# Gated linear attention: the levels' gaps, decays, splits and unit copies in another order, one pair ahead

## What is computed

```python
def gla_mixer(h, w_in, w_gate2, b_gate, o_norm_g, w_out):
    q, k, v, g, lr = split(h @ w_in)            # 4 heads, dk 128, dv 256; lr: 2 x 16 gate columns
    la_f, la_b = log_sigmoid(lr_d @ w_gate2[d] + b_gate[d]) / 16      # decays, forwards and backwards
    o_f = gla(q / sqrt(128), k, v, la_f)                              # o_i = sum_{j<=i} (q_i exp(b_i - b_j)) . k_j v_j
    o_b = flip(gla(flip q, flip k, flip v, flip la_b, strict))        # the same from behind, j > i
    return (rms_norm(o_f + o_b, o_norm_g) * silu(g)) @ w_out          # b = cumsum(log decay)
```

## Time and profile before

| | |
|---|---|
| median of 3 runs | 1629.79 us (1622.76 to 1631.01) |
| the profiled execution | 1620.01 us, its span 1618.2 us |
| mean granted TensorE clock | 0.957 of full speed |
| busy in the span | TensorE 1481.0 us (92%), VectorE 904.5, ScalarE 663.8, GpSimd 154.2 |
| the attention stage | 228.1 to 413.9 us of the span |

### The profile page before, as it was taken

One profiled execution on the slowest core, in us unless ns is written; L12 is line 12 of the kernel. 1 busy time (PEld: TensorE's weight loads), 2 busy tenths in 40 slices (PEclk: granted clock), 3 DMA queues, 4 the chain that ended last, 5 costly groups with the idle time before them and its releaser, 6 DMA issues.

```text
span 1618.2 us, 23133 instructions
## 1 busy us (share of the span) xinstructions
PE 1481.0 (92%) x10100; PEld 1361.7 (84%) x10100; DVE 904.5 (56%) x976; ACT 663.8 (41%) x750; POOL 154.2 (10%) x148
## 2 busy tenths in 40 slices
PE   4999988888999999999989567999999997899997
PEld 3999987887899998999979546999988785699996
DVE  3677657664556645565544654546555556455443
ACT  3433335343444334333344443444435444343332
POOL 2000000661000000000030402000014000100000
PEclk9999998999999999999999778999999997999999
DMA  6777534131576645676466202555544111245551
GB/s 218 260 237 258 172 101 149 60 105 62 193 249 239 243 161 200 242 251 218 156 133 210 102 1 71 205 187 180 182 143 131 53 53 53 64 157 191 186 182 53
DMA packets 175523, 255.39 MB, mean 158 GB/s; under 512 B 4707, under 2 KB 153486, under 8 KB 172350
## 3 DMA queue, kind: packets, MB, share of 16 engines
q1 hardware_dynamic: 173168, 248.59, 45.6%
q0 software_dynamic: 1968, 5.22, 1.6%
q10 hardware_dynamic: 286, 0.09, 0.0%
HBM read 252.57 MB, written 1.31 MB: 157 GB/s over the span
## 4 chain that ended last, share of the span: by engine, by line
PE 81%; DVE 7%; POOL 5%; ACT 3%; DMA 2%; issue 2%; SPq 0%; DVEq 0%; POOLq 0%; ACTq 0%
PE bank L179 16%; PE bank L180 16%; PE bank L181 16%; PE acc L179 8%; PE acc L180 8%; PE acc L181 8%; DVE w_lo L159 1%; POOL arena L757 1%; PE acc L874 1%; ACT w_hi L153 1%; PE bank L1239 1%; PE acc L1915 1%; POOL rstd L782 1%; PE bank L1939 1%; POOL arena L756 1%
## 5 line engine op out<-in xcount | busy, mean ns | idle before, releaser
L159 DVE TENSOR_TENSOR w_lo<-w_raw,w_hi 128x2048 fp32r<-128x2048 f32 x212 | 489.2, 2309 | 372.6 <-ACT w_hi L153 372.4
L179 PE MATMUL bank<-h_hi,w_hi 128*128 128x256 f32 x1848 | 530.6, 287 | 6.6 <-DVE h_lo L270 5.1
L180 PE MATMUL bank<-h_lo,w_hi 128*128 128x256 f32 x1848 | 529.3, 286 | 0.0
L181 PE MATMUL bank<-h_hi,w_lo 128*128 128x256 f32 x1848 | 529.1, 286 | 0.0
L153 ACT ACTIVATE w_hi<-w_raw 128x2048 fp32r<-128x2048 f32 x212 | 403.9, 1908 | 294.9 <-PE bank L181 239.4
L179 PEld LDWEIGHTS bank<-h_hi,w_hi 128*128 128x128 f32 x1848 | 359.7, 195 | 12.3 <-issue 10.1
L180 PEld LDWEIGHTS bank<-h_lo,w_hi 128*128 128x128 f32 x1848 | 359.6, 195 | 2.2
L181 PEld LDWEIGHTS bank<-h_hi,w_lo 128*128 128x128 f32 x1848 | 359.4, 194 | 0.6
L179 PE MATMUL acc<-w_hi,act_hi 128*128 128x512 f32 x408 | 159.5, 391 | 1.5 <-DVE act_lo L444 1.5
L180 PE MATMUL acc<-w_lo,act_hi 128*128 128x512 f32 x408 | 159.4, 391 | 0.0
L181 PE MATMUL acc<-w_hi,act_lo 128*128 128x512 f32 x408 | 158.7, 389 | 0.0
(11 more groups left out here) (288 smaller groups left out, 1714.4 us busy)
## 6 DMA issues: line engine op xcount, KB each, us to landing
w_raw<-in_ffn_w_gu SPq DMA_DIRECT2D x88, 1024.0 KB, 5.1
w_raw<-in_ffn_w_down SPq DMA_DIRECT2D x44, 1024.0 KB, 4.9
arena<-in_w_ada SPq DMA_DIRECT2D x24, 1024.0 KB, 5.8
w_raw<-in_w_ffn_in SPq DMA_DIRECT2D x22, 1024.0 KB, 5.1
w_raw<-in_gla_w_in SPq DMA_DIRECT2D x12, 1024.0 KB, 5.4
w_raw<-in_diff_w_in SPq DMA_DIRECT2D x12, 1024.0 KB, 5.7
w_raw<-in_w_ffn_out SPq DMA_DIRECT2D x11, 1024.0 KB, 5.1
w_raw<-in_w_in SPq DMA_DIRECT2D x9, 1024.0 KB, 5.1
```

The lines of the kernel that those rows point to most:

```text
L159: eng.tensor_tensor(w_lo[:, slot, :], w_raw[:, slot, :], w_hi[:, slot, :].bitcast(F32), ALU.subtract).then_inc(sem("unit_split"), 1)
L179: pe.matmul(out_, a[0], b[0], start=first, stop=False)
L180: pe.matmul(out_, a[0], b[1], start=False, stop=False)
L181: return pe.matmul(out_, a[1], b[0], start=False, stop=last)
```

## The change

The same instructions are issued, in another order. On TensorE unit 1 moves in front of the logits and unit 5 in front of the levels, so that the unit behind a pair is the next higher one and the last pair has none. On ScalarE split 4 and Ln stand in front of the copy of unit 1, the copy of a unit in front of the next high split (from n = 6), and the two decays of a pair on both sides of them. On VectorE gap 0 stands between the two directions' sums and gap 1 behind them; then, for each pair, both gaps of the next pair, one low split and the pair's copies follow each other. The log decays (`gla_la`) move from the region of the weighed buffers to that of g, so that the first weighing needn't wait for the sums, and the first copy of g (unit 5) does.

```diff
--- before.py
+++ after.py
@@ -521,7 +521,7 @@
         GLA_COL = [2 * GLA_QK + 2 * GH * GDV + 2 * GRANK - P, 0, UC, GLA_QK, GLA_QK + UC]
         GLA_COL += [2 * GLA_QK + GH * GDV + n * UC for n in range(4)] + [2 * GLA_QK + n * UC for n in range(4)]
         N_GLA_IN = len(GLA_COL)
-        gla_la = region(0, 2, GH * S)
+        gla_la = region(12288, 2, GH * S)
         gla_u = region(0, 2, GH * S)
         gla_b = region(2048, 2, 2, GH * S)
         gla_gap = region(6144, 2, GH * S)
@@ -562,10 +562,8 @@
             u = base[name]
             stage_norm_scalar(eng, name)
 
-            def unit(n):
-
-                if n + 3 < N_GLA_IN + 4:
-                    split_hi(eng, u + n + 3)
+            def copied(n):
+
                 eng.wait_ge(sem("unit_used"), gla_unit_done(n))
                 b = bank[n % 2]
                 if n == 0:
@@ -580,8 +578,17 @@
                     eng.activation(dst[:, :, c:c + UC], b[:, :].rearrange("p (t c) -> p t c", t=TT), ACT.Copy)\
                         .then_inc(sem("gla_copied"), 1)
 
+            def decay(s):
+
+                m, _, _, _ = gla_level(s)
+                eng.wait_ge(sem("gla_gap"), s + 1)
+                e = gla_blocks(gla_gap[:, s % 2, :], m)
+                for c, sign in ((slice(0, m), -1.0), (slice(m, 2 * m), 1.0)):
+                    eng.activation(e[:, :, c], e[:, :, c], ACT.Exp, scale=sign / GNORM).then_inc(sem("gla_decay"), 1)
+
             split_hi(eng, u + 2)
-            unit(0)
+            split_hi(eng, u + 3)
+            copied(0)
             for z in range(8):
                 if z % 2 == 0:
                     eng.wait_ge(sem("gla_logits"), z // 2 + 1)
@@ -591,28 +598,30 @@
             for d in range(2):
                 eng.wait_ge(sem("gla_abs"), 4 * d + 4)
                 eng.activation(gla_abs[:, d, :], gla_abs[:, d, :], ACT.Exp, scale=-1.0).then_inc(sem("gla_exp"), 1)
-            unit(1)
+            split_hi(eng, u + 4)
             for d in range(2):
                 eng.wait_ge(sem("gla_exp"), d + 1)
                 eng.activation(gla_abs[:, d, :], gla_abs[:, d, :], ACT.Ln, bias=1.0).then_inc(sem("gla_softplus"), 1)
-            unit(2)
-            unit(3)
-            unit(4)
-
-            def decay(s):
-
-                m, _, _, _ = gla_level(s)
-                eng.wait_ge(sem("gla_gap"), s + 1)
-                e = gla_blocks(gla_gap[:, s % 2, :], m)
-                for c, sign in ((slice(0, m), -1.0), (slice(m, 2 * m), 1.0)):
-                    eng.activation(e[:, :, c], e[:, :, c], ACT.Exp, scale=sign / GNORM).then_inc(sem("gla_decay"), 1)
-
+            copied(1)
+            for n in (2, 3):
+                split_hi(eng, u + n + 3)
+                copied(n)
             decay(0)
+            copied(4)
+            split_hi(eng, u + 7)
             decay(1)
-            for s in range(1, GLA_STEPS, 2):
-                for n in range(s + 1, min(s + 3, GLA_STEPS)):
-                    decay(n)
-                unit(5 + s // 2)
+            decay(2)
+            eng.wait_ge(sem("gla_sums"), 4)
+            copied(5)
+            split_hi(eng, u + 8)
+            decay(3)
+            for n in range(6, N_GLA_IN):
+                if 2 * n - 8 < GLA_STEPS:
+                    decay(2 * n - 8)
+                copied(n)
+                split_hi(eng, u + n + 3)
+                if 2 * n - 7 < GLA_STEPS:
+                    decay(2 * n - 7)
 
             eng.wait_ge(sem("gla_copied"), 9)
             for t in range(TT):
@@ -642,17 +651,18 @@
                 eng.wait_ge(sem("gla_ones"), kind + 1)
                 starts = gla_reset[:, kind, :].rearrange("p (n w) -> p n w", w=width)[:, :, 0:1]
                 eng.memset(starts, 0.0).then_inc(sem("gla_reset"), 1)
-            split_lo(eng, u + 2)
-            split_lo(eng, u + 3)
-            for z in range(8):
-                if z % 2 == 0:
-                    eng.wait_ge(sem("gla_abs"), z + 2)
-                eng.tensor_scalar(gla_la[:, z // 4, (z % 4) * S:(z % 4 + 1) * S],
-                                  acc_bank[z // 2][:, (z % 2) * S:(z % 2 + 1) * S],
-                                  cols[:, COL_BG + z:COL_BG + z + 1], 0.0, ALU.add, ALU.min)\
-                    .then_inc(sem("gla_min"), 1)
-            split_lo(eng, u + 4)
-            for d in range(2):
+            def gap(s):
+                m, backwards, kind, mid = gla_level(s)
+                if s < 2:
+                    eng.wait_ge(sem("gla_sums"), 2 * s + 2)
+                else:
+                    eng.wait_ge(sem("gla_weighted"), s - 1)
+                b = gla_blocks(gla_b[:, backwards, kind, :], m)
+                eng.tensor_tensor(gla_blocks(gla_gap[:, s % 2, :], m), b,
+                                  b[:, :, mid:mid + 1].broadcast_to([P, GH * S // (2 * m), 2 * m]),
+                                  ALU.subtract).then_inc(sem("gla_gap"), 1)
+
+            def sums(d):
                 eng.wait_ge(sem("gla_softplus"), d + 1)
                 eng.wait_ge(sem("gla_min"), 4 * d + 4)
                 eng.tensor_tensor(gla_la[:, d, :], gla_la[:, d, :], gla_abs[:, d, :], ALU.subtract)\
@@ -664,31 +674,11 @@
                         eng.tensor_tensor_scan(gla_b[:, d, kind, :], gla_reset[:, kind, :], gla_la[:, d, :], 0.0,
                                                ALU.mult, ALU.add).then_inc(sem("gla_sums"), 1)
                     else:
-                        earlier = region(GH * S - 1, GH * S)
+                        earlier = region(12288 + GH * S - 1, GH * S)
                         eng.tensor_tensor_scan(gla_b[:, d, kind, :], earlier, gla_reset[:, kind, :], 0.0,
                                                ALU.add, ALU.mult).then_inc(sem("gla_sums"), 1)
-                split_lo(eng, u + 5 + d)
-            split_lo(eng, u + 7)
-
-            def gap(s):
-                m, backwards, kind, mid = gla_level(s)
-                if s == 0:
-                    eng.wait_ge(sem("gla_sums"), 4)
-                if s >= 2:
-                    eng.wait_ge(sem("gla_weighted"), s - 1)
-                b = gla_blocks(gla_b[:, backwards, kind, :], m)
-                eng.tensor_tensor(gla_blocks(gla_gap[:, s % 2, :], m), b,
-                                  b[:, :, mid:mid + 1].broadcast_to([P, GH * S // (2 * m), 2 * m]),
-                                  ALU.subtract).then_inc(sem("gla_gap"), 1)
-
-            gap(0)
-            gap(1)
-            eng.wait_ge(sem("gla_own"), 1)
-            for t in range(TT):
-                eng.tensor_copy(gla_s[:, t, t, :], bank[2 + t][:, :]).then_inc(sem("gla_kept"), 1)
-            for s in range(GLA_STEPS):
-                if s + 2 < GLA_STEPS:
-                    gap(s + 2)
+
+            def kept(s):
                 m, backwards, kind, mid = gla_level(s)
                 eng.wait_ge(sem("gla_scores"), s + 1)
                 if m < P:
@@ -701,8 +691,34 @@
                 else:
                     eng.tensor_copy(gla_s[:, backwards, 1 - backwards, :], acc_bank[2 * (s % 2)])\
                         .then_inc(sem("gla_kept"), 2)
-                if s % 2:
-                    split_lo(eng, u + 8 + s // 2)
+
+            split_lo(eng, u + 2)
+            split_lo(eng, u + 3)
+            for z in range(8):
+                if z % 2 == 0:
+                    eng.wait_ge(sem("gla_abs"), z + 2)
+                eng.tensor_scalar(gla_la[:, z // 4, (z % 4) * S:(z % 4 + 1) * S],
+                                  acc_bank[z // 2][:, (z % 2) * S:(z % 2 + 1) * S],
+                                  cols[:, COL_BG + z:COL_BG + z + 1], 0.0, ALU.add, ALU.min)\
+                    .then_inc(sem("gla_min"), 1)
+            split_lo(eng, u + 4)
+            sums(0)
+            split_lo(eng, u + 5)
+            gap(0)
+            sums(1)
+            split_lo(eng, u + 6)
+            gap(1)
+            eng.wait_ge(sem("gla_own"), 1)
+            for t in range(TT):
+                eng.tensor_copy(gla_s[:, t, t, :], bank[2 + t][:, :]).then_inc(sem("gla_kept"), 1)
+            split_lo(eng, u + 7)
+            for p in range(GLEVELS):
+                for s in (2 * p + 2, 2 * p + 3):
+                    if s < GLA_STEPS:
+                        gap(s)
+                split_lo(eng, u + 8 + p)
+                kept(2 * p)
+                kept(2 * p + 1)
 
             eng.wait_ge(sem("gla_out"), 2)
             for h in range(GH):
@@ -746,7 +762,6 @@
                 pool.wait_ge(sem("gla_decay"), 2 * s + 2)
                 if s == 0:
                     pool.wait_ge(sem("gla_copied"), 5)
-                    pool.wait_ge(sem("gla_sums"), 4)
                 if s >= 2:
                     pool.wait_ge(sem("gla_scores"), s - 1)
                 e, u_ = gla_blocks(gla_gap[:, s % 2, :], m), gla_blocks(gla_u[:, s % 2, :], m)
@@ -841,6 +856,7 @@
                 last.then_inc(sem("unit_used"), 1)
 
             unit(0)
+            unit(1)
             pe.wait_ge(sem("gla_copied"), 1)
```

(7 more changed lines are left out.)

## The result

| | before | after |
|---|---|---|
| median (the runs of this comparison) | 1628.13 us (4 runs) | 1603.07 us (4 runs, 1599.37 to 1606.93) |
| ratio | | 0.985, 95% interval 0.981 to 0.989 |
| profiled execution, its span | 1620.01, 1618.2 us | 1603.81, 1602.0 us |
| attention stage in the profile | 185.8 us | 166.4 us |
| outside the stage | 1432.4 us | 1435.6 us |

Faster, as forecast, in the main by the forecast's mechanism, and by more: 25 us between these medians, where 15 was forecast.

A forecast was written before the change was run, and what follows sets the result against it. It took the attention stage to be bound by waits among GpSimd, TensorE, VectorE and ScalarE, not transfers. Terms -12.9 - 9.1 + 1.8 + 3.7 + 1.5 = -15.0 us, off the 1629.8 median, gave about 1615 us; range 1606 to 1626.

The forecast's parts named there:

- First term: Front and start of the levels: unit 6 ends at 292.8 instead of 305.68 us, -12.9 us.
- the 1.4 us set aside for the clock there: Start of the levels: added to unit 6's end for a lower clock after 4.1 us of idle before scores 1.
- the idle ahead of unit 3 is covered: Front: TensorE's new 4.2 us idle costs nothing, covered by the 4 us wait before scores 1.
- Second and third term: Levels: six pairs in 58.5 instead of 67.6 us, -9.1; VectorE and GpSimd meeting on the SBUF port, +1.8 us.
- The loop through VectorE and ScalarE: Levels: gaps, decay, copy, high and low split and predicated copies set each pair's period, 9.75 us.
- the third term: Levels: split and weighing meeting on the SBUF port cost 0.3 us a pair, +1.8 us.
- The wait that was to go: Levels: the slow pair's waits, with gap and weighing no longer behind the split, should go.
- Fourth and fifth term: End: outputs start 6.2 instead of 2.54 us after unit 12, +3.7; outputs possibly at 1.2 GHz, +1.5 us.
- (a): Levels: split and weighing meet on the path every pair, period stays 11.3 us; 7.5 us less won, 1622; chance 0.13.
- (b): Three new idles of 4 us bring 10 us stretches at 1.2 GHz; 1624 to 1628 us; chance 0.11.
- (c): Levels: low split ahead of predicated copies makes the loop 13.95 us, slower at 1638 us; chance 0.05.
- (d): Something else holds the stage's end, so no effect, 1630 us; chance 0.04.

The follow-up runs named there:

- warm: Changed kernel with 16 unread identity products behind unit 2 and 16 ahead of the outputs; ratio 0.983 on the kernel before, stage 167.7 us.
- split_behind: Changed kernel with the low split behind the predicated copies in every pair, gaps still one pair ahead; ratio 0.984 on the kernel before, stage 160.5 us.
- end_swapped: Changed kernel with only the last low split moved behind the last two copies of scores; ratio 0.985 on the kernel before, stage 161.8 us.
- gap1_first: Changed kernel with gap 1 ahead of low split 6 on VectorE; ratio 0.986 on the kernel before.
- before_warm: Kernel before with unread identity products in seven of TensorE's idles; ratio 0.994 on the kernel before, stage 183.9 us.
- front_only: Kernel before with one edit, unit 1 ahead of the logits on TensorE; ratio 0.998 on the kernel before, stage 187.1 us.
- after_again: Changed kernel timed again without an edit; ratio 0.983 on the kernel before.

## Where the prediction was right, and where it was not

**First term, -12.9; measured -14.5** (unit 6 ends 63.1 instead of 77.6 us after the stage's start). The times of the front were met within 2 us: TensorE came 1.7 us later to scores 0 (for the low stretch in unit 3) and scores 1 started 0.4 us earlier, so the wait ahead of scores 1 was 1.91 us, not 4.1, and the 1.4 us set aside for the clock there weren't spent. That the idle ahead of unit 3 is covered holds (warm).

**Second and third term, -9.1 and +1.8; measured -10.2 together.** The loop through VectorE and ScalarE takes 9.55 us, not 9.75, and the port adds nothing on the path: the third term is 0. The wait that was to go has gone, and the even pairs have come. The reason given, that gaps and weighing no longer stand behind the split, was put too widely: they still do in the program's order, but behind a split whose unit was done a pair earlier (split_behind). split_behind also shows that the loop isn't the bound in the other order, where TensorE's 9.33 us nearly are.

**Fourth and fifth term, +3.7 and +1.5; measured +3.6 and +1.7.** Met. end_swapped gives both back, all but 0.8 us.

**The sum, -15.0; measured -19.4** between the first two profiles of the stage. The third term (1.8 too much), the loop (1.1) and the first term (1.6) are the difference. All three erred to one side, towards caution.

**The anchor.** The forecast median was 1614.8 us, the measured one 1603.1, 11.7 lower. The terms make 4.4 of that, and with them right the forecast would have been 1629.8 - 19.4 = 1610.4, still inside the range. The step that put the result outside is the last one: a gain worked out inside one profiled execution was taken off a median of three others, as if it were the same in them. It makes the other 7.3: 1.7 because that median was high (1628.1 with the fourth run), and 5.6 because 25.1 us lie between the medians, where the first two profiles differ by 19.4. The lower end of the range had 4 us for it.

Of the 5.6 the profiles show 0.9: the stage takes 187.5 us on the mean of before's five and 167.2 in three of the changed kernel, -20.3. In before the difference to the first profile's 185.8 is low clock that the first was spared: in unit 0 in three of the others, at one more slow pair and the outputs in the long one. I took before's clock as the first profile had it, and priced only the new idles.

How much of the 20.3 is clock can be read from TensorE's busy time, for the same 1106 products: 160.2 us on the mean of the five stages (158.6 to 163.3 each), 153.4 on that of the three (151.6 to 155.8). So 6.8 us, a third, is work at a higher clock, and 13.5 are idle time that is gone.

**What stays open.** The mean of 61 runs of before is 1627.4 us, that of fifteen of the changed kernel 1604.0: 23.4 us, with a 95% interval of 21.3 to 25.6 from their scatter (standard deviations 4.8 and 3.5). The profiles explain 20.3 of it in the stage, and nothing outside (1434.4 and 1434.2 us on the mean). Before's five profiled executions were short ones, 1623.8 us on the mean; the three of the changed kernel took 1603.2. So the missing 3 us lie in executions that no profile shows, and means of five and three can't tell 3 us from chance. The clock speaks for more low stretches in before: the mean granted clock of the whole execution is 0.951 in the 52 other runs of before that have it on record, and 0.955 in the five profiled ones. Among those 52 the time falls with the clock, by some 10 us for each 0.01 (correlation -0.82), which would make about 4 us of the difference between the two groups; the changed kernel has 0.957 in all fifteen as in the three. Where in the kernel these stretches lie is not shown.

Also open is what unit 5's new place on TensorE does without ScalarE's new order.

**The rivals.** (a), the port keeps the old period: wrong, 9.6 against 11.3 us. (b), the clock takes the gain back: a fall at the outputs cost 1.7 us here (8.83 for 7.17) and some 3 in other executions (10.1 in that of gap1_first), not 5.2, and over all the clock went the other way, by 6.8 us in the stage. The change takes more idle time away than it adds, 27.3 us in the stage before and 13.8 after. (The Trainium skill, "TensorE: Matmul & The Clock Gate", section "Why this matters for your kernels", warns of idles between bursts: the outputs at 0.81 of full clock behind 3.84 us of idle bear it out, and so do before_warm's 9 us, for the kernel before.) (c), the split ahead of the copies: it costs 0.7 us over six pairs, and some 5 at the end. (d), no effect: wrong.

## What to carry to other kernels

Where a step stands behind a split or a load for no need of its own, move it one round ahead, or the work that the split itself waits for; look then at the last round, where the order that fitted the loop may have nothing left to hide behind. Short waits of TensorE that recur cost more than their length, since behind some of them the clock is down, and not behind the same ones in each execution: count the idles that could, not those that did in one profile. And before a gain from one profile is taken from a median, ask how that execution stands to the others: two more profiles of the unchanged kernel would have shown that its stage was 1.2 us short, and the granted clocks of the other executions that its clock was high.

## What the runs showed of the hardware, not expected

The clock fell right behind the eight logit products though TensorE had been busy without a break: in front_only they ran from 244.24 to 247.96 behind 8.8 us of full work, and the clock stood at 0.54 for the next 3.7 us. It was so in eight of the ten profiles with unit 1 directly ahead of them, not in the changed kernel's first. In after_again the stretch behind them is

```profile
247.71:251.75 4.04, 4.04 (x21) 4.04 (x22) 1.78 (x5) 3.99 (x6) 0.00 (x0) 0.58 0.53 167
```

These products use 32 rows of the array, the others 128; whether that is the cause no run tests. A part of the low stretch behind before's logits need not come from the idle ahead of them: in before_warm, with that idle filled, the clock fell behind them all the same.

Products of the identity put into an idle kept the clock up at the outputs of warm (7.15 against 8.83 us), and there was no fall at the three slow pairs of before_warm, but one ahead of its second scores.
